# Two-layer hybrid decoder: the first loads on two DMA queues, and expert matrices read in one run per partition

## The chip, the cores and the metric

The kernel runs on one core of one Trainium2 chip. The metric is the device time of one execution in microseconds (us), from the runs listed below. The profile is one further execution, recorded by the hardware profiler. The engines are TensorE (PE, its weight loads PEld), VectorE (DVE), ScalarE (ACT), GpSimd (POOL) and SyncE (SP). SP, ACT and POOL each have a queue of their own into the core's 16 DMA engines, shown as q1, q10 and q0 in the profile.

## What is computed

Two layers over 512 tokens of 1024 features, all float32. Each layer has a mixer (sliding-window attention and an mLSTM, fed by one input projection) and a mixture of experts: 16 experts with 512 hidden features each, two of them per token. Both halves are preceded by a norm that a conditioning vector `c` modulates.

```python
mod = silu(c) @ ada_w[l] + ada_b[l]
sh1, sc1, g1, sh2, sc2, g2 = split(mod, 6)
h = rms_norm(x, norm_mix_w[l]) * (1.0 + sc1) + sh1
...                                    # mixer: x = x + g1 * (merged @ w_out[l])
h2 = rms_norm(x, norm_ffn_w[l]) * (1.0 + sc2) + sh2
# router: best group, then the best 2 experts e in it, weights gate
y = (silu(h2 @ w_gate[l, e]) * (h2 @ w_up[l, e])) @ w_down[l, e]
x = x + g2 * sum_over_2_experts(gate * y)
```

## The kernel before

Everything is written out by hand for each engine, with semaphores between them.

**The head** (before the loop over layers). SP issues the vector `c`, the positions and the router bias (L413 to L416), the first 2 MB block of `ada_w` (`load_head(0)`, L419), the router's matrix in two pieces (L429), then `params(0)`: 18 small loads through `rows` (L391), and then `x` (L431), the three other blocks of `ada_w` (L419) and the matrices of the `q` and `kv` projections (L424). ACT issues nothing here. DVE waits for all five constants (`const_in`), works out sine and cosine arguments (L1337 to L1359), ACT takes their sines (L666), then the silu of `c` (L669), and then squares and scales the four token tiles of `x` (L673, L678). PE transposes `c` (L948), waits for DVE and ACT, and in `param_columns(0)` waits for all 18 parameter loads, transposes the parameter rows (L967) and goes through `head_mods`: for each of four blocks of `ada_w` a product (L979), whose row ACT copies (L694) and whose columns PE sums (L961). Then the modulated tiles are transposed (L1020) and the `q` products start (L1030).

**The mixer** streams further blocks of `ada_w` through DVE (L1452, L1454); their sums are turned into columns on PE, for the chunks 6 to 9 by `paired_sums` (L955, four products of 128 columns). After the output projection (L1208) DVE writes the normed tokens `xn` (L1698), PE transposes them (L1216), and the router follows.

**The experts.** Tokens are scattered by expert into rows in DRAM and processed in blocks of 64 rows; an expert has one block or more. For a block PE does gate and up products (L1260), the transposes of the next block's rows (L1252), the down product of the block before (L1272) and the transposes of the hidden rows (L1266). DVE multiplies silu(gate) by up (`hx`, L1821) and scales the result (`y_row`, L1808). ACT issues the loads of the rows of later blocks (L887, 256 KB) and the stores of the result (L898, two of 128 KB). There are three buffers of weights: SP issues gate (L484) and up (L487) of expert e once the last gate and up product of expert e-3 is done, and POOL issues down (L617, or L619 and L620) once its last down product is done. Each is 2 MB:

```python
wait_reg(sp, gu_ready, blocks_through(sp, e - BUF))
load_gate(p, e)
load_up(p, e)
...
dve.wait_ge(y_out, b * 32 + 32)     # y_row of block b: the store of block b - 1 has landed
```

Gate and up are laid out by pairs of features (`of_pairs`): a partition holds four runs of 4 KB, 512 KB apart in DRAM. Down is laid out by `of`: four rows of 4 KB, also 512 KB apart. `wo` denotes the output projection, `gb` and `yb` gate and up products of the mLSTM branch.

## Time and profile before

| | |
|---|---|
| median of 3 runs | 1703.74 us (1700.13 to 1704.67) |
| the profiled execution | 1704.2 us, its span 1702.6 us |
| PE busy | 1488.8 us (87%) |
| DVE, ACT, POOL busy | 642.8, 324.3, 126.8 us |
| mean granted PE clock | 0.944 |
| DMA | 383.34 MB, 225 GB/s over the span |
| blocks of 64 rows | 46 in both layers |

How to read it: busy PE is not PE at its peak, and the share is a mean over stages with different limits. The head (0 to 51 us) and parts of the expert stages (553 to 848 and 1374 to 1677 us) are where PE waits for transfers; "granted clock" is PE's, 1.00 for 2.4 GHz and 0.50 for 1.2 GHz.

### The profile page before, as it was taken

How to read it: one execution, taken by the hardware profiler on the slowest of the kernel's cores; microseconds unless marked ns; L12 is line 12 of the kernel's file. 1: busy time of each engine (PE TensorE's matmuls, PEld its weight loads, DVE VectorE, ACT ScalarE, POOL GpSimd, SP SyncE). 2: the span in 40 equal slices, each digit the busy share in tenths (PEclk: the TensorE clock that was granted, in tenths of full speed). 3: DMA queues.
4: the chain of work that ended last, by engine and by line, in shares of the span. 5: the costliest groups of instructions: out<-in, count | busy, mean ns of one | idle time of the engine just before them, and what ended most of it. 6: DMA issues, size and time to landing. Idle time of an engine off the chain costs nothing.

```text
span 1702.6 us, 18332 instructions
## 1 busy us (share of the span) xinstructions
PE 1488.8 (87%) x5723; PEld 666.5 (39%) x5724; DVE 642.8 (38%) x1573; ACT 324.3 (19%) x825; POOL 126.8 (7%) x165
## 2 busy tenths in 40 slices
PE   2999999989992899989759999999999558999993
PEld 0544445544441333323234444454444223333331
DVE  1346434557524122112144554365763411121223
ACT  3223421100001112112143242111000111121220
POOL 1100000001102000000031000000110110000002
PEclk9999999999996799999979999999999869999997
DMA  8961112367706699999766012126773479996895
GB/s 265 386 249 49 51 50 84 114 249 294 279 18 247 183 347 392 379 389 390 267 236 221 1 50 86 62 99 232 262 253 142 152 271 381 392 387 230 304 383 181
DMA packets 140466, 383.34 MB, mean 225 GB/s; under 512 B 18760, under 2 KB 20984, under 8 KB 140408
## 3 DMA queue, kind: packets, MB, share of 16 engines
q1 hardware_dynamic: 107224, 273.04, 44.0%
q0 software_dynamic: 21664, 83.89, 13.1%
q10 hardware_dynamic: 11520, 25.70, 4.9%
q8 instruction: 29, 0.48, 0.1%
q14 instruction: 29, 0.24, 0.0%
HBM read 346.95 MB, written 35.65 MB: 225 GB/s over the span
## 4 chain that ended last, share of the span: by engine, by line
PE 74%; DMA 10%; DVE 5%; issue 5%; ACT 2%; POOL 1%; SPq 1%; POOLq 0%; ACTq 0%; DVEq 0%
PE bank L1041 23%; PE bank L1260 17%; PE bank L1030 11%; PE bank L1272 8%; PE bank L1208 5%; DMA weight_ring<-in_w_up_dram 4%; DMA regA<-in_w_up_dram 2%; PE bank L1252 1%; DMA h_features<-in_ada_w_dram 1%; DMA expert_rows<-merged_features 1%; PE bank L1108 1%; SPq L391 1%; PE bank L1266 1%; PE bank L1097 1%; POOL expert_rows L636 1%
## 5 line engine op out<-in xcount | busy, mean ns | idle before, releaser
L1041 PE MATMUL bank<-h_features,weight_ring 128*128 128x512 f32 x768 | 345.2, 603 | 2.0 <-ACT regB L756 2.0
L1260 PE MATMUL bank<-weight_ring,merged_features 128*64 128x512 f32 x960 | 224.9, 623 | 14.6 <-DMA weight_ring<-in_w_up_dram 7.5
L1041 PEld LDWEIGHTS bank<-h_features,weight_ring 128*128 128x128 f32 x768 | 146.7, 194 | 183.8 <-issue 183.5
L1030 PE MATMUL bank<-weight_ring,h_features 128*128 128x512 f32 (+1 forms) x512 | 196.3, 541 | 0.7 <-DVE h_features L1403 0.7
L1821 DVE TENSOR_TENSOR merged_features<-bank,merged_features 64x512 f32<-64x512 f32 x44 | 30.5, 693 | 364.2 <-ACT merged_features L890 364.2
L1030 PEld LDWEIGHTS bank<-weight_ring,h_features 128*128 128x128 f32 x512 | 95.9, 190 | 94.8 <-issue 90.7
L1260 PE MATMUL bank<-h_features,merged_features 128*64 128x512 f32 x256 | 116.7, 610 | 18.0 <-DMA regA<-in_w_up_dram 17.0
L1260 PEld LDWEIGHTS bank<-weight_ring,merged_features 128*64 128x64 f32 x960 | 72.1, 143 | 143.6 <-issue 138.9
L1272 PE MATMUL bank<-weight_ring,merged_features 128*64 128x512 f32 x528 | 120.6, 598 | 1.6 <-DVE merged_features L1808 1.6
L1260 PE MATMUL bank<-regA,merged_features 128*64 128x512 f32 x256 | 117.2, 612 | 0.0
L1208 PE MATMUL bank<-weight_ring,merged_features 128*128 128x512 f32 x256 | 114.3, 608 | 3.0 <-POOL merged_features L614 3.0
L890 ACT ACTIVATE merged_features<-bank 64x512 f32<-64x512 f32 x46 | 27.1, 590 | 351.3 <-PE bank L1260 351.3
L1208 PEld LDWEIGHTS bank<-weight_ring,merged_features 128*128 128x128 f32 x256 | 49.5, 195 | 64.7 <-issue 61.5
L881 ACT ACTIVATE merged_features<-bank,mod_cols,scale 128x64 f32<-128x64 f32 x192 | 62.2, 404 | 63.4 <-PE bank L1252 61.2
L1252 PE MATMUL bank<-ident,merged_features 64*128 64x64 f32 x384 | 34.9, 233 | 43.3 <-DMA merged_features<-expert_rows 43.3
L1260 PEld LDWEIGHTS bank<-h_features,merged_features 128*64 128x64 f32 x256 | 34.7, 141 | 80.5 <-issue 80.5
L1808 DVE TENSOR_TENSOR merged_features<-bank,g_rows 128x512 f32<-128x512 f32 x46 | 31.8, 691 | 88.0 <-PE bank L1272 83.0
L1804 DVE TENSOR_SCALAR merged_features<-bank,scale,mod_cols 128x64 f32<-128x64 f32 x192 | 52.8, 337 | 31.9 <-PE bank L1252 30.3
L1252 PEld LDWEIGHTS bank<-ident,merged_features 64*128 64x128 f32 x384 | 28.2, 142 | 80.8 <-DMA merged_features<-expert_rows 43.5
L1041 PE MATMUL bank<-regB,weight_ring 128*128 128x512 f32 x128 | 57.9, 595 | 1.6 <-DVE regB L1672 1.6
L1272 PEld LDWEIGHTS bank<-weight_ring,merged_features 128*64 128x64 f32 x528 | 35.4, 136 | 60.1 <-issue 58.0
L1041 PE MATMUL bank<-regA,weight_ring 128*128 128x512 f32 x128 | 57.7, 594 | 0.0
(319 smaller groups left out, 1456.6 us busy)
## 6 DMA issues: line engine op xcount, KB each, us to landing
weight_ring<-in_w_gate_dram SPq DMA_DIRECT2D x22, 2048.0 KB, 12.7
weight_ring<-in_w_up_dram SPq DMA_DIRECT2D x22, 2048.0 KB, 18.9
weight_ring<-in_w_down_dram POOLq DMA_DIRECT2D x22, 2048.0 KB, 16.7
weight_ring<-in_w_in_dram SPq DMA_DIRECT2D x18, 2048.0 KB, 17.7
x_tokens<-in_ada_w_dram SPq DMA_DIRECT2D x14, 2048.0 KB, 8.0
h_features<-in_w_gate_dram SPq DMA_DIRECT2D x10, 2048.0 KB, 11.4
regA<-in_w_up_dram SPq DMA_DIRECT2D x10, 2048.0 KB, 20.2
regA<-in_ada_w_dram SPq DMA_DIRECT2D x8, 2048.0 KB, 8.0
```

The source lines that it names most:

```text
L391: sp.dma_start(dst, src).then_inc(params_in, 16)
L881: last = ac.activation(xT[:, k, :], ps[2][:, MB * k:MB * k + MB], ACT.Identity, scale=A2[:, k:k + 1], bias=modc[:, 24 + k:25 + k])
L890: ac.activation(hsil[64:P, :], ps[3][0:64, :], ACT.Silu).then_inc(sil_ready, 1)
L1030: ins = te.matmul(bank[:, 0:w], hT[:, k, P * i:P * i + P], wv[:, k, :], start=(k == 0), stop=(k == KD - 1))
L1041: ins = te.matmul(bank[:, :], wv[:, k, c0:c0 + P], rhs[:, k, :], start=(k == 0), stop=(k == kn - 1))
L1208: ins = te.matmul(bank[:, :], merged[:, k, P * i:P * i + P], slot(f"wo{k // 4}", 4, D)[:, k % 4, 512 * h:512 * h + 512], start=(k == 0), s ...
L1252: ins = te.transpose(ps[(2, 6)[k % 2]][:, MB * k:MB * k + MB], xg[p][:, P * k:P * k + P], ident[MB * p:MB * p + MB, MB * p:MB * p + MB])
L1260: ins = te.matmul(ps[3][64 * part:64 * part + 64, :], xT[:, k, :], w[:, k, :], start=(k == 0), stop=(k == KD - 1))
L1272: ins = te.matmul(ps[5][64 * half:64 * half + 64, :], hxT[:, k, :], down_w[p][k][:, 512 * half:512 * half + 512], start=(k == 0), stop=(k ...
L1804: last = ve.tensor_scalar(xT[:, k, :], ps[6][:, MB * k:MB * k + MB], A2[:, k:k + 1], modc[:, 24 + k:25 + k], ALU.mult, ALU.add)
L1808: ve.tensor_tensor(yb, ps[5][:, :], g2bc[:, :], ALU.mult).then_inc(y_taken, 1)
L1821: ve.tensor_tensor(hx, ps[3][64:P, :], hsil[64:P, :], ALU.mult).then_inc(hx_ready, 1)
```

## The change

It has four parts. First, in the head, SP issues only `c`, the four blocks of `ada_w`, `q` and `kv`; ACT issues the positions, `x`, the router bias, the router's matrix and the parameters, 16 loads now, before its own first activation. Second, gate, up and down are read so that partition p holds the K consecutive rows pK to pK+K-1 of the matrix: one run of 16 KB (down of buffer 1: runs of 12 and 4 KB). Third, what is multiplied by them is written in the same order: `hx` with a stride of 4 elements on both inputs, `xn` with a stride of 8 (it was 2), and the columns of the modulation in chunks 6 to 9 by eight products of 64 columns. Fourth, the parameters of the second norm are loaded as columns straight away (three loads of 128 x 8), so the transposed rows are 68 and not 128.

```diff
-        def of_pairs(w, l, e):
-            return w.rearrange("l e (m p r) f -> (l e) p m (r f)", p=P, r=2)...
+        def whole_rows(w, l, e, k):
+            return w.rearrange("l e (p k) f -> (l e) p (k f)", k=k)[bass.ds(l * E + e, 1)].rearrange("a p n -> p (a n)")
...
-            load_head(0)
-            sp.wait_ge(zeroed, 2)
-            for r in range(2):
-                sp.dma_start(rwz[:, r:KD:2, 0:E], router_w.rearrange("(m p r) e -> p m r e", p=P, r=2)[:, :, r, :])...
-            params(0)
-            sp.dma_start(xs[:, :, :], x.rearrange("a (i p) d -> p (a i) d", p=P)).then_inc(x_in, 16)
-            for j in range(1, HEAD_ADA):
+            for j in range(HEAD_ADA):
                 load_head(j)
             for name in ("q", "kv"):
                 load(0, name)
...
-                    sp.dma_start(gate_w[p].rearrange("p (m r) n -> p m (r n)", r=2), of_pairs(w_gate, l, e))...
+                    sp.dma_start(gate_w[p].rearrange("p k n -> p (k n)"), whole_rows(w_gate, l, e, KD))...
...
-                        po.dma_start(ring[:, (2, 1, 5)[p], :].rearrange("p (k n) -> p k n", k=FC), of(w_down, l, e))...
+                        po.dma_start(ring[:, (2, 1, 5)[p], :], whole_rows(w_down, l, e, FC)).then_inc(w_dn[p], 16)
...
         def _(act):
             ac = nc.scalar
 
+            with nc.allow_non_contiguous_dma(reason="positions by token"):
+                act.dma_start(rt[:, 0:NT].bitcast(I32), positions...).then_inc(const_in, 16)
+            act.dma_start(xs[:, :, :], x.rearrange("a (i p) d -> p (a i) d", p=P)).then_inc(x_in, 16)
+            act.dma_start(rbias[:, :], router_bias...).then_inc(const_in, 16)
+            act.wait_ge(zeroed, 1)
+            act.dma_start(rwz[:, :, 0:E], router_w.rearrange("(p k) e -> p k e", p=P)).then_inc(const_in, 16)
+            params(act, 0)
             act.wait_ge(dve_const, 1)
             ac.activation(sinr[:, :, :]...
...
+            def row_column_sums(bank, half, rows):
+                for k in range(KD):
+                    ins = te.matmul(bank[64 * half:64 * half + 64, k:k + 1], rows.rearrange("t (p k) -> t k p", k=KD)[:, k, :],
+                                    ones[:, 0:1], start=True, stop=True)
...
-                    ve.tensor_scalar(xn[:, i, :].rearrange("t (m r p) -> t m r p", r=2, p=P), xs[:, i, :].rearrange("t (m p r) -> t m r p", p=P, r=2),
+                    ve.tensor_scalar(xn[:, i, :].rearrange("t (k p) -> t k p", p=P), xs[:, i, :].rearrange("t (p k) -> t k p", k=KD),
                                      rs[:, 4 + i:5 + i], None, ALU.mult).then_inc(xn_ready, 1)
...
+                def hidden():
+                    by_row = lambda a: a.rearrange("t (p k) -> t k p", k=FC)
+                    ve.tensor_tensor(hx.rearrange("t (k p) -> t k p", p=P), by_row(ps[3][64:P, :]), by_row(hsil[64:P, :]), ALU.mult).then_inc(hx_ready, 1)
```

On SP, at the start of the program, before the change (`regP`, `rbias` and `router_padded` take the constants, `weight_ring` and `h_features` the blocks of `ada_w`):

```order
L413 DMA regP<-in_c_dram 8x128
L415 DMA regP<-in_positions_dram 128x4x1
L416 DMA router_bias<-in_router_bias_dram 128x16
L419 DMA weight_ring<-in_ada_w_dram 128x8x512
L429 DMA router_padded<-in_router_w_dram 128x4x16 x2
L391 DMA regP<-in_norm_mix_w_dram 8x128
...
L391 DMA gate_columns_padded<-in_w_in_dram 128x8x4 x2
L431 DMA x_tokens<-in_x_dram 128x4x1024
L419 DMA weight_ring<-in_ada_w_dram 128x8x512 x2
L419 DMA h_features<-in_ada_w_dram 128x8x512
```

And the same place of SP after it:

```order
L406 DMA regP<-in_c_dram 8x128
L410 DMA weight_ring<-in_ada_w_dram 128x8x512 x3
L410 DMA h_features<-in_ada_w_dram 128x8x512
L415 DMA weight_ring<-in_w_in_dram 128x8x512
L415 DMA weight_ring<-in_w_in_dram 128x8x256
```

All constants but `c`, `x` and every parameter have left SP, so that the four blocks of `ada_w` follow each other at once.

On ACT, the start of the program after the change (before it ACT began with the table load and the sine, and issued nothing):

```order
L649 DMA regP<-in_positions_dram 128x4x1
L650 DMA x_tokens<-in_x_dram 128x4x1024
L651 DMA router_bias<-in_router_bias_dram 128x16
L653 DMA router_padded<-in_router_w_dram 128x8x16
L381 DMA regP<-in_norm_mix_w_dram 8x128
...
L381 DMA g_rows<-in_ada_b_dram 128x1024
L381 DMA qk_norm_rows<-in_q_norm_w_dram 128x64
...
L381 DMA param_cols<-in_ada_b_dram 128x8 x2
...
L381 DMA gate_columns_padded<-in_w_in_dram 128x8x4 x2
L656 ACT_TABLE_LOAD
L656 ACTIVATE sin<-regP 128x32
```

`x` now stands ahead of the router's matrix and of all parameters, and ACT's first activation behind all of these issues.

## Rows read from the trace of the kernel before

**Rows 1.** Busy time by stretch, 10 to 20 us; last: clock, DMA share, GB/s.
```profile
10.00:20.00 10.00, 0.27 (x1) 0.18 (x1) 5.28 (x35) 1.82 (x4) 0.00 (x0) 1.00 0.58 73
```

**Rows 2.** Timeline of the head: start, us, engine, line, tiles, [idle before <-releaser].
```profile
11.26 0.17 DVE L1337 CAST regP<-regP 128x4 f32<-128x4 int32 x1 [11.26 <-DMA router_padded<-in_router_w_dram]
...
18.04 1.52 SPq L431 DMA_DIRECT2D x_tokens<-in_x_dram  x1
...
20.60 0.45 PE L967 MATMUL bank<-ident,regP 128*128 128x128 f32 x1 [9.05 <-DMA gate_columns_padded<-in_w_in_dram]
...
21.49 3.64 PE L979 MATMUL bank<-weight_ring,c_padded 128*32 128x512 f32 x16 [0.44 <-DVEq L1391]
...
27.00 1.06 ACT L673 ACTIVATE merged_features<-x_tokens 128x1024 f32<-128x1024 f32 x1 [8.74 <-DMA x_tokens<-in_x_dram]
...
36.52 1.05 PE L961 MATMUL bank<-ones,regU 128*128 128x1 f32 x8 [0.44 <-ACT regU L694]
...
37.87 1.92 PE L979 MATMUL bank<-weight_ring,c_padded 128*32 128x512 f32 x16 [0.30 <-DMA weight_ring<-in_ada_w_dram]
...
43.30 3.39 PE L979 MATMUL bank<-h_features,c_padded 128*32 128x512 f32 x16 [2.51 <-DMA h_features<-in_ada_w_dram]
```

**Rows 3.** The chain that ended last: start, us, what.
```profile
51.08 7.10 PE bank L1030 x16
...
712.25 3.58 PE bank L1272 x16
```

**Rows 4.** DMA queues, 18 to 21 us, SP's queue with short packets: packets, MB, share.
```profile
q1 hardware_dynamic: 2316, 0.12, 64.0%
```

**Rows 5.** DMA queues, 30 to 40 us, SP's queue alone with runs of 2 KB.
```profile
q1 hardware_dynamic: 1920, 3.87, 105.1%
```

**Rows 6.** DMA queues, 749 to 751 us, runs of 4 KB: SP's, then POOL's.
```profile
q1 hardware_dynamic: 104, 0.43, 53.3%
q0 software_dynamic: 96, 0.39, 49.1%
```

**Rows 7.** DMA queues, 778 to 779 us, ACT's queue with stores of 2 KB.
```profile
q0 software_dynamic: 43, 0.18, 42.8%
q1 hardware_dynamic: 39, 0.16, 38.9%
q10 hardware_dynamic: 43, 0.09, 22.6%
```

**Rows 8.** PE's waits, experts of layer 1 and then 2: us in total, times, longest.
```profile
PE bank L1260 <- DMA regA<-in_w_up_dram: 10.2, 2, 7.9
PE bank L1260 <- DMA weight_ring<-in_w_up_dram: 7.5, 2, 5.9
...
PE bank L1260 <- DMA regA<-in_w_up_dram: 6.7, 1, 6.7
```

**Rows 9.** SP's timeline of issues, and the landing time of the issue at 793.74.
```profile
641.65 0.38 SPq L484 DMA_DIRECT2D weight_ring<-in_w_gate_dram  x1
...
793.74 8.35 SPq L487 DMA_DIRECT2D weight_ring<-in_w_up_dram  x1
...
weight_ring<-in_w_up_dram SPq DMA_DIRECT2D x1, 2048.0 KB, 35.4
...
1389.38 0.38 SPq L484 DMA_DIRECT2D weight_ring<-in_w_gate_dram  x1
```

**Rows 10.** The chain that ended last, layer 2: the wait for up of expert 5.
```profile
1414.78 33.68 DMA regA<-in_w_up_dram
```

**Rows 11.** Timeline, two blocks: result rows and ACT's stores.
```profile
739.38 0.69 DVE L1808 TENSOR_TENSOR merged_features<-bank,g_rows 128x512 f32<-128x512 f32 x1 [1.78 <-PE bank L1272]
...
740.32 1.13 ACTq L898 DMA_DIRECT2D expert_rows<-merged_features  x2
...
751.02 0.69 DVE L1808 TENSOR_TENSOR merged_features<-bank,g_rows 128x512 f32<-128x512 f32 x1 [1.79 <-PE bank L1272]
```

**Rows 12.** One line's instructions: ns min/median/max, first and last start.
```profile
L1698 DVE TENSOR_SCALAR regA<-x_tokens,rstd x8: 752/754/754, 471.8 to 1335.6; 128x1024 f32<-128x1024 f32 x8
```

More of the change, by code:

```diff
@@ L424, in load @@
                 sp.dma_start(dst, src).then_inc(item_in[name], 16)
-            load_head(0)
-            sp.wait_ge(zeroed, 2)
-            for r in range(2):
-                sp.dma_start(rwz[:, r:KD:2, 0:E], router_w.rearrange("(m p r) e -> p m r e", p=P, r=2)[:, :, r, :]).then_inc(const_in, 16)
-            params(0)
-            sp.dma_start(xs[:, :, :], x.rearrange("a (i p) d -> p (a i) d", p=P)).then_inc(x_in, 16)
-            for j in range(1, HEAD_ADA):
+            for j in range(HEAD_ADA):
                 load_head(j)
@@ L945, in _ @@
             te = nc.tensor
-            pe.wait_ge(const_in, 16 * 5)
+            pe.wait_ge(const_in, 16 * 4)
             pe.wait_ge(pool_const, 2)
@@ L950, in _ @@
             pe.wait_ge(dve_const, 3)
-            def paired_sums(bank, rows):
-                for q in range(4):
-                    ins = te.matmul(bank[:, q:q + 1], paired(rows, q), ones[:, 0:1], start=True, stop=True)
-                return ins
             def column_sums(bank, rows):
@@ L962, in column_sums @@
                 return ins
+            def row_column_sums(bank, half, rows):
+                for k in range(KD):
+                    ins = te.matmul(bank[64 * half:64 * half + 64, k:k + 1], rows.rearrange("t (p k) -> t k p", k=KD)[:, k, :],
+                                    ones[:, 0:1], start=True, stop=True)
+                return ins
             def param_columns(t):
-                wait_head(pe, params_in, t, 18 * 16, 18 * 16)
-                te.transpose(ps[2][:, 0:P], prm[:, :], ident[:, :]).then_inc(param_cols, 1)
+                wait_head(pe, params_in, t, 16 * 16, 16 * 16)
+                te.transpose(ps[2][:, 0:68], prm, ident[0:68, 0:68]).then_inc(param_cols, 1)
             def head_mods():
```

92 lines of the change are left out of this document (42 added, 50 removed).

## The prediction, made before the change was run

> **What bounds the kernel now.** I read the busy time by stretch first, then the chain that ended last, then the timeline of the head and PE's waits in the experts, and last the DMA queues. From 10 to 20 us PE works 0.27 us and DMA moves 73 GB/s [rows 1]: the short parameter loads fill SP's queue. PE's first real work waits for the last of them at 20.6 us, and later steps wait for `x` (27.0) and for blocks of `ada_w`, the fourth at 43.3 [rows 2]; the `q` products start at 51.08 [rows 3]. That is the first place. The second is the experts: a block takes 11.64 us of PE (from 739.38 to 751.02) [rows 11], and where experts with one block follow each other their 6 MB come too late. PE waits 17.7 us in layer 1 and 6.7 in layer 2 for an up matrix [rows 8]. Between these places the mixer is PE's own, and no part of the change reaches it but the column sums.
>
> **Prices of packets.** With SP's queue alone and runs of 2 KB, 1920 packets take 105.1% of 160 us, 87.6 ns each [rows 5]. Runs of 4 KB take 53.3% of 32 us over 104, 164 ns each [rows 6]. On a straight line through both, a packet of 16 KB takes 622 ns against 4 x 164 = 656: 5.1% less per byte. Packets under 512 B: 64.0% of 48 us over 2316, 13 ns each [rows 4]. Two queues get one packet each in turn (104 and 96) [rows 6], three as well (43, 39, 43), although ACT's are of 2 KB there and the others of 4 [rows 7]. So the turn goes by packets, not by bytes.
>
> **The head.** Before, 18 parameter loads and the router's 2 stood ahead of `x` and three blocks. Now SP's queue has the four blocks at once, 64 packets of 2 KB for each block and engine, and ACT's has the rest. What was one queue of 13 ns packets is now one whose every packet takes a turn with a 2 KB packet: 88 + 13 = 101 ns. I count ACT's packets for each of 16 engines, from the shapes in the order shown: `x` 32 of 4 KB; then router bias 8, router matrix 64 (128 x 8 pieces), parameter rows 4, `g1` 8 of 4 KB, the two norms 16, sinks 8, three columns 24, gate columns 128. `x` is issued at about 1.5 us; before, it took from 18.04 to 27.0 us for 32 x 0.164 = 5.2 us of packets, so some 2 us go by before its first packet. From 3.5 us: `x` 32 x (0.088 + 0.164) = 8.1; the 260 others x 0.101 = 26.3, plus 1.2 for the 4 KB ones, plus about 2, an estimate, for one short packet that ends each load, plus 1 to be seen: parameters complete at **42 us**, against 20.6 [rows 2]. If a 13 ns packet slips in beside the long one for nothing, 260 x 0.088 gives 38.5; if every landing is as late as `x`'s was, 44. I take 42.
>
> The fourth block has landed by then: all that goes before it is 256 x 0.0876 + 5.2 for `x` + 1.3 + some 4 of short ones + 3.5 + 1 = 37.8 us. The constants end behind 72 of ACT's turns, near 20 us (before 11.3), and DVE's 5 us after them still end before 42. ACT issues until about 30 us and then has its sines, a table load and 9 us of squares and scaling, which also ends near 42. So the chain from the parameters on decides: 0.9 to the first block's product, 3.64, then about 2.9 for the second (3.64 on the low clock, 1.92 on the high), a column sum 1.0, third 1.92, column sum 1.0, and from the start of the fourth 7.8 - 1.5 = 6.3 (51.08 - 43.30, less 3.39 - 1.92) [rows 2, 3]: 17.7 us. `q` starts at 59.8: **+8.7 us**. Bounds +5 and +11.
>
> **The experts.** SP's queue in layer 1 is filled from 641.65 on: each later pair is issued before the pair ahead has landed, up to the up matrix issued at 793.74, which lands at 829.1 [rows 9]. 5.1% of these 187.5 us is 9.6. In layer 2 the same holds from 1389.38 to 1448.5 [rows 9, 10]: 3.0. Gain 12.6 us, of the 24.4 waited. As ends: nothing, if packets gain nothing, and 31 us, all of the waits and an estimate of 7 for the products behind them that run at the low clock (3.64 against 1.92 for the same product) [rows 2].
>
> Some is given back. By turns, ACT's rows pay for the long packets: a block has 4 packets of loaded rows, 8 of stores and 3 that end a load or store, per engine, 15 turns. With SP and POOL both full, a turn is 2 x 0.622 us, and 15 take 18.7 + 1.4 us against the block's 11.64; with SP alone 10.7. `y_row` waits for the store of the block before. The store is issued at 740.32, the next `y_row` came at 751.02 [rows 11] and could slip to about 758 before PE's down product waits: 17 us of slack, of which 4 go by before a first packet. Its 9 turns take 11.9 us with both full, 7.1 with one, and loaded rows can stand ahead. POOL's 32 packets of 4 KB per expert, each beside one of SP's, fill 32 x 0.328 = 10.5 us of the 16.7 that an expert takes (46 blocks over 32 experts, 11.64 each), so I take 5.6 us given back, and 0 and 17 as ends. **-7.0 us** in sum, bounds -31 and +5.
>
> **The rest.** `xn` reads with a stride of 8 elements. With stride 2 the 1024 elements took 754 ns [rows 12], faster than one per DVE cycle; I take half a microsecond more, for the last tile of each layer (the others hide under the output projection): +1.0, bounds 0 and +2. The Trainium skill, SBUF — State Buffer, on cachelines (16 bytes there, 8 in PSUM, a line to be hit twice), speaks against all strided reads here; by it the 0.754 us could double, +1.5 in sum, and no row here has such a stride. The `hx` product hides under PE's down product of 3.58 us [rows 3], in which ACT's silu and DVE's evacuation of the next block's rows (both about a microsecond) lie too; so it could take some 1.5 to 2 us more, and costs 0. The column sums, 8 calls, have twice the products of half the columns, 1.05 us before [rows 2]: 0, and 0 and +7 as ends. The next layer's parameters lose their 4-byte pieces in the shadow of the experts: 0; if SP were late there, gate of expert 3 would come later.
>
> **Sum:** +8.7 - 7.0 + 1.0 = +2.7 on 1704.2 (span 1702.6 and 1.6 around it) is 1706.9. The median of the runs stands 0.5 lower, so **1706.5 us**. A measurement of this kernel tells 0.3%, 5.1 us, from no change.
>
> **Rivals.**
> *Short packets don't take a turn each.* If a queue gives several short ones per turn, parameters are in at about 26 us and the fourth block at 37.8 decides instead of 43.3: -5.5. With -7.0 and +1.0 that is 1692.5. For it: nothing shows short packets in turn with long ones. Against: ACT's 2 KB stores got one per turn, not two for one of 4 KB [rows 7]. The Trainium skill, DMA: Bandwidth & Descriptors, "Queues, rings and completion order", says an engine drains a whole packet of typically 9 to 17 descriptors before it switches; by that this rival would hold. Rows 7 don't bear it out for 2 KB.
> *Rows starve behind long packets* (the other side). If 16 KB gain nothing (656 ns), the turn with both queues full is 1.31 us, the store needs 4 + 9 x 1.4 = 16.6 of its 17 us, and any loaded rows ahead of it make `y_row` late in most blocks from 641 to 829 us. It decides once a turn passes 1.4 us. Experts +5, head +8.7, rest +1: 1718.
> *The runs are not one packet.* If the queue cuts 16 KB into packets of 4 as before, nothing moves in the experts: +8.7 + 1.0, 1713.5. Against: no run here was longer than 4 KB, so nothing either way.
>
> **How the numbers follow.** Forecast 0.50, first rival 0.28, second 0.13, third 0.09. The forecast's own range is -4 to +12: 0.04 faster, 0.30 within 0.3%, 0.16 slower. The first rival is faster but for 0.01 (0.27); the second and third are slower but for 0.01 of the third. Sums: faster 0.31, same 0.32, slower 0.37. For 8 in 10 the range reaches 5.5 us below the first rival and just past the second: 1687 to 1719, with some 0.1 left out on either side.
>
> **What would show it.** Right: the parameters' transpose between 38 and 44 us with DMA near 390 GB/s from 4 us on, the first `q` product at 57 to 62; packets of 16 KB in the queues, about 620 ns each; the up waits smaller, DVE idle before `y_row` on DMA. Wrong: a transpose before 30 us (first rival); waits of `y_row` above 5 us in sum beside unchanged waits for up (second); no packet above 4 KB (third). If `hx` takes over 2.5 us, a term I left at nothing is the bound of every block, and the prediction fails.

## The result, and the profile after

Four runs of the changed kernel took 1743.12 us in the median (1737.07 to 1744.21), beside 1703.57 us for the kernel before on the same chip: ratio 1.0228, 95% interval 1.0201 to 1.0256. It is 39 us slower, where 1706.5 had been forecast and 1719 was the upper end. The profiled execution, the fastest of the four, took 1737.07 us, span 1735.5, granted clock 0.947.

The span is 32.9 us longer. Cut at PE's first product of each stage, it lies here (us; in brackets PE's granted clock over the stage):

| stage, up to | before | after | difference |
|---|---|---|---|
| head, first `q` product | 51.1 | 58.0 | +6.9 |
| mixer 1, first output product | 401.2 (0.99) | 406.9 (0.98) | +5.7 |
| router 1, first gate product | 106.9 | 106.3 | -0.6 |
| experts 1, first transpose of layer 2 | 309.0 | 313.2 | +4.2 |
| mixer 2 | 405.8 (0.98) | 411.4 (0.97) | +5.6 |
| router 2 | 105.8 | 104.6 | -1.2 |
| experts 2, end | 322.8 | 335.1 | +12.3 |

Each column is one execution, and stages scatter. Over these two profiles and those of the experiments that share the code of a stage, the experts took 304.3 to 309.0 us before and 310.3 to 314.6 after in layer 1, and 321.5 to 322.8 and 334.4 to 336.9 in layer 2; `q` started at 51.1 to 54.5 us before and at 57.7 to 59.0 after.

**The head** is close to the forecast. The timeline of the head after the change (start, us, engine, line, tiles, idle before and its releaser):

```profile
21.37 0.17 DVE L1328 CAST regP<-regP 128x4 f32<-128x4 int32 x1 [21.37 <-DMA router_padded<-in_router_w_dram]
...
41.69 0.35 PE L958 MATMUL bank<-ident,regP 68*128 68x68 f32 x1 [20.02 <-DMA gate_columns_padded<-in_w_in_dram]
...
42.41 5.47 PE L970 MATMUL bank<-weight_ring,c_padded 128*32 128x512 f32 x32 [0.38 <-DVEq L1382]
...
57.96 2.38 PE L1021 MATMUL bank<-weight_ring,h_features 128*128 128x512 f32 x5 [0.71 <-ACT h_features L674]
```

The parameters' transpose starts at 41.69 us (20.60 in [rows 2]; 42 forecast), `q` at 57.96 (59.8 forecast). The two queues in this time (packets, MB, share of 16 engines), 20 to 30 us and then 30 to 40:

```profile
q1 hardware_dynamic: 1506, 3.02, 83.7%
q10 hardware_dynamic: 1505, 0.63, 24.6%
...
q1 hardware_dynamic: 1735, 3.48, 98.3%
q10 hardware_dynamic: 1676, 0.03, 11.7%
```

ACT's packets, of some 20 bytes each in the second stretch (0.03 MB in 1676), take turns one for one with SP's of 2 KB. Equal counts over 10 us could also come of equal groups. But in three stretches of 0.21 us from 34.00 us on (two turns of each of the 16 engines) the two queues moved 38 and 38, 34 and 34, 39 and 40 packets; with groups of nine or more these counts would scatter by a dozen (an estimate). The Trainium skill, DMA: Bandwidth & Descriptors, "Queues, rings and completion order", has an engine drain a whole packet of typically 9 to 17 descriptors before it switches. The trace does not agree: these counts show single turns, and refute the first rival.

**The experts.** PE's waits for up matrices (24.4 us in [rows 8]) are gone. DVE waits in their place; its largest wait for transfers (us in total, times, longest), and then all DMA from 640 to 830 us, before and after:

```profile
DVE merged_features L1804 <- DMA expert_rows<-merged_features: 147.3, 20, 13.9
...
DMA packets 20391, 73.55 MB, mean 387 GB/s; under 512 B 1299, under 2 KB 1299, under 8 KB 20391
...
DMA packets 8445, 73.35 MB, mean 386 GB/s; under 512 B 1225, under 2 KB 1225, under 8 KB 4419
```

L1804 is `y_row`, which waits for the store of the block before: 147.3 us over 20 blocks, against 4.9 us once before. From 714 to 716 us a packet of 16 KB takes 0.61 us (29 packets fill 55.4% of 32 us), as I had extrapolated:

```profile
q1 hardware_dynamic: 29, 0.48, 55.4%
q0 software_dynamic: 22, 0.36, 42.0%
...
q1 hardware_dynamic: 64, 1.05, 84.7%
q10 hardware_dynamic: 64, 0.26, 19.9%
```

From 706 to 710 us, though, where ACT's queue loads rows and POOL's is empty, the same packet takes 0.85 us. So the rate over the filled stretch did not rise by the forecast 5.1%: it is 386 GB/s, before 387. In this stretch of layer 1 DMA is full in both kernels, and one wait was exchanged for another. In the first 120 us of the experts of layer 2 the rate fell, from 364 to 355 GB/s. The chain that ended last, after the change, layer 1, shows what a block is made of (start, us, what):

```profile
705.53 0.70 DVE merged_features L1804
...
707.12 15.47 DMA expert_rows<-merged_features
722.61 0.70 DVE merged_features L1804
...
724.21 17.35 DMA expert_rows<-merged_features
741.58 0.70 DVE merged_features L1804
```

`y_row`, its store, the store's landing, the next `y_row`: a ring of 17.1 and 19.0 us, where a block of [rows 11] took 11.64. The chain has eleven such rounds in the two layers, of 13.6 to 19.2 us; their stores took 12.0 to 17.6 us to land.

**Blocks that wait for no transfer** are longer too. The chain in layer 2 after the change:

```profile
1634.61 0.39 PE bank L1257 x4
1635.00 0.45 issue
1635.45 7.09 PE bank L1251 x32
```

Two in three of these blocks take 12.0 to 12.2 us, the others 11.75. Their 0.3 to 0.49 us of "issue", in which PE waits for nothing that the profile shows, were 0.15 at most before (a third of the blocks at 11.77 us, the others at 11.63).

**The strided operations and the mixer.** One line each (ns min/median/max, first and last start): `hx` before and after, then `xn`, then the weight loads of the column sums; and one call of these on the timeline of the mixer, before and after; last, PE over a stretch behind another call (us, PE busy, granted clock, DMA share, GB/s):

```profile
L1821 DVE TENSOR_TENSOR merged_features<-bank,merged_features x44: 692/693/695, 583.8 to 1668.8; 64x512 f32<-64x512 f32 x44
...
L1801 DVE TENSOR_TENSOR merged_features<-bank,merged_features x46: 1045/1080/1102, 580.9 to 1703.1; 64x512 f32<-64x512 f32 x46
...
L1690 DVE TENSOR_SCALAR regA<-x_tokens,rstd x8: 1142/1150/1156, 484.4 to 1355.7; 128x1024 f32<-128x1024 f32 x8
...
L951 PEld LDWEIGHTS bank<-ones,regU x96: 194/217/220, 287.8 to 1178.3; 128*64 128x64 f32 x96
...
280.85 1.00 PE L955 MATMUL bank<-ones,regU 128*128 128x1 f32 x8
...
287.80 2.08 PE L951 MATMUL bank<-ones,regU 128*64 128x1 f32 x16
...
1179.40:1182.80 3.40, 3.40 (x5) 0.50 0.00 0
```

`hx` takes 1.08 us (0.69 before), `xn` 1.15 (0.754 in [rows 12]). A column sum takes 2.08 us; before, with four products of 128 columns, it took 1.00 (each product is two instructions). Eight sums make 8.6 us of the 11.3 that the mixers grew by. The granted clock has the rest: PE was at its low level for 13.6 us of each mixer, before for 10.2. The fall at 1179.4 us comes 0.8 us behind a column sum. Twice 3.4 us at half speed are 3.4 us, an estimate, so 12.0 us together.

### The profile page after: what moved, and what is told of

It is laid out like the page before. It is cut to its first block, busy times and chain, and to the rows that moved or that the text cites. A ratio compares the mean times of both kernels' runs of the same rounds, so it can differ in the third digit from the quotient of the medians.

```text
span 1735.5 us, 18454 instructions
## 1 busy us (share of the span) xinstructions
PE 1502.1 (87%) x5787; PEld 687.0 (40%) x5788; DVE 663.8 (38%) x1573; ACT 323.9 (19%) x825; POOL 119.3 (7%) x164
## 4 chain that ended last, share of the span: by engine, by line
PE 70%; DMA 13%; issue 6%; DVE 6%; ACT 2%; POOL 2%; ACTq 1%; POOLq 0%; DVEq 0%
PE bank L1032 23%; PE bank L1251 14%; PE bank L1021 11%; DMA expert_rows<-merged_features 10%; PE bank L1263 7%; PE bank L1199 5%; DMA gate_columns_padded<-in_w_in_dram 1%; PE bank L1243 1%; ACTq L381 1%; PE bank L1099 1%; DMA regA<-expert_rows,slot_index 1%; PE bank L1088 1%; PE bank L951 1%; DVE merged_features L1804 1%; POOL expert_rows L619 1%
## 5 line engine op out<-in xcount | busy, mean ns | idle before, releaser
L1801 DVE TENSOR_TENSOR merged_features<-bank,merged_features 64x512 f32<-64x512 f32 x46 | 49.7, 1081 | 290.0 <-ACT merged_features L880 290.0
L1251 PEld LDWEIGHTS bank<-weight_ring,merged_features 128*64 128x64 f32 x960 | 79.1, 140 | 133.0 <-issue 129.2
L1804 DVE TENSOR_TENSOR merged_features<-bank,g_rows 128x512 f32<-128x512 f32 x46 | 31.8, 691 | 184.2 <-DMA expert_rows<-merged_features 147.3
L1263 PEld LDWEIGHTS bank<-weight_ring,merged_features 128*64 128x64 f32 x528 | 38.7, 144 | 83.0 <-issue 81.3
L1032 PE MATMUL bank<-regA,weight_ring 128*128 128x512 f32 x128 | 61.2, 623 | 0.0
## 6 DMA issues: line engine op xcount, KB each, us to landing
weight_ring<-in_w_in_dram SPq DMA_DIRECT2D x18, 2048.0 KB, 12.7
```

The lines of the kernel that those rows point to most:

```text
L1032: ins = te.matmul(bank[:, :], wv[:, k, c0:c0 + P], rhs[:, k, :], start=(k == 0), stop=(k == kn - 1))
L1251: ins = te.matmul(ps[3][64 * part:64 * part + 64, :], xT[:, k, :], w[:, k, :], start=(k == 0), stop=(k == KD - 1))
L1263: ins = te.matmul(ps[5][64 * half:64 * half + 64, :], hxT[:, k, :], down_w[p][k][:, 512 * half:512 * half + 512], start=(k == 0), stop=(k ...
L1801: ve.tensor_tensor(hx.rearrange("t (k p) -> t k p", p=P), by_row(ps[3][64:P, :]), by_row(hsil[64:P, :]), ALU.mult).then_inc(hx_ready, 1)
L1804: ve.tensor_tensor(yb, ps[5][:, :], g2bc[:, :], ALU.mult).then_inc(y_taken, 1)
```

## The experiments

Each ran beside the kernel before. Differences between experiments are differences of these ratios, times 1703.6 us; by their intervals such a difference is uncertain by 6 to 10 us. "After" is the changed kernel.

**The head put back.**

```diff
...
+            load_head(0)
+            sp.wait_ge(zeroed, 1)
+            sp.dma_start(rwz[...], router_w...)
+            params(sp, 0)
+            sp.dma_start(xs[...], x...)
-            for j in range(HEAD_ADA):
+            for j in range(1, HEAD_ADA):
```

(positions and router bias ahead of these, and all of them taken off ACT)

> Only the head is put back: positions, router bias, router matrix, the 16 parameter loads and x go to SP again, in the order of before, and ACT issues nothing there. Theory (parameters are late because each short packet of ACT's takes a turn with a 2 KB packet of SP's): the parameters' transpose comes at 18 to 22 us and not at 41.7, q starts at 50 to 52 us and not at 57.96, and the whole gets 7 us shorter than after, since nothing behind the head sees it: about 1736. Rival (the head costs nothing in the end, because what is late there is made up in the mixer, whose weights come no sooner): q is earlier but the time stays within 2 us of after's.

Measured 1732.67 us, ratio 1.0181 (1.0149 to 1.0214): 8.0 us less than after. The parameters' transpose came at 18.55 us and `q` at 46.71, earlier than before's 51.08. By 20 us SP's queue had moved 6378 packets, before's 8708; that this is why was not tested. The 11.3 us by which `q` is earlier than after's came out as 8, so most of what the head loses stays lost, as forecast.

**All short loads first, on both queues.**

```diff
             sp.dma_start(crow, ...)
...
+            params(sp, 0, (0,))          # rows, norms, sinks, three columns
             for j in range(HEAD_ADA):
...
-            act.dma_start(xs[...], x...)
             act.dma_start(rbias...); act.dma_start(rwz...)
-            params(act, 0)
+            params(act, 0, (1,))         # gate columns, gate biases, g1
+            act.dma_start(xs[...], x...)
```

> After, but in the head all short loads stand ahead of the long ones on both queues: SP c, the parameter rows, norms, sinks and the three columns, then the four blocks of ada; ACT positions, router bias, router matrix, gate columns, gate biases, g1, then x. Theory (turns): while only short packets are in both queues a turn costs 2 x 13 ns, the parameters are complete at 8 to 12 us, the fourth block at 35 to 37, q starts at 44 to 46 us, 12 to 14 less than after's: about 1730. Rival (short loads cost by the load, some microseconds each to land, not by the turn): parameters not before 20 us, q not before 50, at most 8 us less.

Measured 1727.61 us, ratio 1.0145 (1.0113 to 1.0178), 14.1 us less than after. The timeline of its head:

```profile
11.92 0.38 PE L962 MATMUL bank<-ident,regP 68*128 68x68 f32 x1 [5.81 <-ACT c_padded L663]
...
22.08 3.45 PE L974 MATMUL bank<-weight_ring,c_padded 128*32 128x512 f32 x16 [9.78 <-DMA weight_ring<-in_ada_w_dram]
```

The parameters are there by 11.92 us, while short packets only meet short ones; PE then waits 9.78 us for the first block of `ada_w`. `q` starts at 46.48 (at 44.4 to 49.9 in the three profiles below that have this head and 16 KB packets). The turn theory holds.

**Packets of 4 KB in the changed layout.**

```diff
-  sp.dma_start(gate_w[p]..., whole_rows(w_gate, l, e, KD)).then_inc(w_gu[p], 16)
+  for b in range(2):
+      sp.dma_start(every_other(gate_w[p]..., b), every_other(whole_rows(w_gate, l, e, KD), b)).then_inc(w_gu[p], 16)
```

(up and down likewise, counts doubled)

> After, but gate, up and down are each read by two DMAs that take every other 4 KB, so that no packet is over 4 KB; layout, strides and head stay. Theory (the result rows wait for the store because each of its packets, and of the loads of rows ahead of it, waits out a 16 KB packet of SP's and one of POOL's): the waits of y_row for the store fall from 147 us to under 20, PE's waits for up matrices come back (15 to 30 us), experts of layer 1 take about 312 us from first gate to first K of the next layer instead of 315.7, those of layer 2 about 12 us less, the whole 15 to 18 us less: about 1726. Rival (the late store comes of the rows' own loads, which keep all queues at 330 GB/s whatever the length of the others' packets): waits of y_row stay over 100 us and the time within 4 us of after's.

Measured 1735.96 us, ratio 1.0203 (1.0150 to 1.0255): only 4 us less, with intervals that overlap, where 15 to 18 were expected. But the waits changed places as the theory said. PE's and DVE's waits for transfers in this run (us in total, times, longest):

```profile
PE bank L1260 <- DMA regA<-in_w_up_dram: 15.0, 2, 10.2
...
DVE merged_features L1813 <- DMA expert_rows<-merged_features: 9.5, 2, 5.0
...
PE bank L1260 <- DMA weight_ring<-in_w_up_dram: 8.5, 2, 4.6
```

From 147.3 us to 9.5 for `y_row`, and 23.5 us for up matrices. Packet length is what makes the store late (it lands in 6.7 us here, in the median). The time hardly followed: PE's waits for matrices are back, and blocks without any wait still took 12.0 us, a second cause beside the first.

**Two buffers for the result rows.**

```diff
-        yb = mflat[:, 3072:3584]
+        yb = [mflat[:, 3072:3584], mflat[:, 3584:4096]]
...
-                    dve.wait_ge(y_out, b * 32 + 32)
+                    with dve.If(b % 2 == 0):
+                        wait_reg(dve, y_out[0], (b // 2) * 32 + 32)
```

> After, but with two buffers for the result rows of a block, so that y_row waits for the store of two blocks before (11.6 us more slack). Theory (only the store is late, loaded rows have slack enough): waits of y_row fall from 147 us to under 40, a block falls from 17 us towards 12 to 14, DMA comes close to 440 GB/s and PE's waits for weights are smaller than before's 24 us; the whole is 15 to 25 us less, 1718 to 1728. Rival (everything that ACT's queue moves is late in the same measure): the waits move to PE's transposes of the next block's rows (L1252), and the time stays within 5 us of after's. A second rival (DMA as a whole is the bound and y_row's waits lie beside it): waits of y_row vanish, PE's waits for up and gate take their place in the same sum, again within 5 us.

Measured 1721.10 us, ratio 1.0119 (1.0087 to 1.0151): 18.6 us less than after, the largest single term; the expert stages are 14.2 us shorter in the profile. Landing times in this run, 640 to 840 us (KB, median us): loads of rows, then stores.

```profile
merged_features<-expert_rows ACTq DMA_DIRECT2D x16, 256.0 KB, 17.0
expert_rows<-merged_features ACTq DMA_DIRECT2D x31, 128.0 KB, 15.9
```

A store takes 15.9 us to land, still, and rows 17.0 (7.2 before). With two buffers the ring may take two blocks; 50.2 us of `y_row`'s waits and 12.7 us more of PE's waits for rows are left.

**Three tests of the longer block.** In the traces of before and after PE's first gate product of a block comes 2.8, 3.1 or 3.2 us after the end of `hx`, where nothing else is late. First, `hx` without strides and PE's transposes reading every fourth column:

```diff
-  ve.tensor_tensor(hx.rearrange("t (k p) -> t k p", p=P), by_row(ps[3][64:P, :]), by_row(hsil[64:P, :]), ALU.mult)
+  ve.tensor_tensor(hx, ps[3][64:P, :], hsil[64:P, :], ALU.mult)
...
-  ins = te.transpose(ps[4][...], hx[:, P * k:P * k + P], ident[0:MB, 0:MB])
+  ins = te.transpose(ps[4][...], hx.rearrange("t (p k) -> t k p", k=FC)[:, k, :], ident[0:MB, 0:MB])
```

> After, but DVE writes hx without strides and PE's four transposes take every fourth column of it instead. In the traces, PE's first gate product of a block starts 1.97 to 2.1 us after DVE's last evacuation of that block's rows, before and after the change alike, and that evacuation stands behind hx on DVE. Theory (this chain sets a block's length, so that hx's 1.10 instead of 0.70 us adds 0.39 us to each): hx takes 0.69 us again, blocks that wait for no transfer fall from 12.02 to 12.15 us back to 11.63 to 11.78, about 26 of them, so 9 to 12 us less than after: 1731 to 1734. Rival (the gap on PE comes of something else in the changed program, such as its instruction stream): blocks stay at 12.0 and the time within 3 us of after's. Should PE's strided weight loads be slower than 138 ns, the transposes of 0.46 us show it.

Measured 1734.32 us, ratio 1.0162 (1.0118 to 1.0206), 11 us less. Blocks take 11.87 us: no "issue" is left, but the transposes' weight loads went from 138 ns to 215:

```profile
L1257 PEld LDWEIGHTS bank<-ident,merged_features x184: 192/215/217, 585.4 to 1707.0; 64*128 64x128 f32 x184
```

`hx` takes 0.69 us again. That the 11 us lie within the 9 to 12 expected was luck in part: the theory had PE wait for the evacuation, which the next two runs refute, and a shorter `hx` helps by either account.

Second, `xt_dve()`, the evacuation of the next block's rows, moved ahead of `hidden()` on DVE; once in after, once in before:

```diff
+                    dve.wait_ge(xt_ready, b + 3)
+                    xt_dve()
                     dve.wait_ge(sil_ready, b + 2)
                     dve.wait_ge(ht_ready, b + 1)
                     hidden()
-                    dve.wait_ge(xt_ready, b + 3)
-                    xt_dve()
```

> After, but DVE evacuates the transposed rows of the next block before it works out hx; nothing else. Theory (PE waits for that evacuation, then its sequencer needs 1.97 us to the first gate product): the evacuation ends 1.1 us earlier, the gap between the hidden rows' transposes and the first gate product falls from 0.77 to 0.39 us or less, blocks to about 11.6 us or a little under, the whole 9 to 14 us less than after. Rival (PE waits for hx, 3.1 us ahead of the gate product, and not for the evacuation): hx now ends 0.7 us later, blocks grow by up to 0.7 us to 12.7 and the whole by 15 us or more.

> The kernel before, with the same exchange: DVE evacuates the next block's transposed rows before it works out hx. Theory (the same chain already sets the block before the change: the gap there is 0.39 to 0.54 us): the gap falls to 0.1 us or less, blocks from 11.63 to about 11.3 us, and, since the stretches that wait for weights take part of it back, 5 to 12 us less than before: 1692 to 1699. Rival (PE's own work fills the block before the change, the 0.39 being its transposes' own length and nothing to win): within 2 us of before.

Measured 1765.79 us, ratio 1.0366 (1.0319 to 1.0412), and 1722.98, ratio 1.0122 (1.0092 to 1.0151). The theory that PE waits for the evacuation fell in both. The chain of the first of the two:

```profile
1640.74 0.39 PE bank L1257 x4
1641.13 1.38 issue
1642.51 7.09 PE bank L1251 x32
```

The "issue" grew by the 1.1 us that `hx` now ends later; the distance from `hx` to the gate product stayed 2.83 to 3.24 us in both kernels, that from the evacuation did not. So PE waits for `hx`, and what follows is most likely its sequencer, since no engine is waited for there. Third, therefore, the wait for `hx` and the transposes behind it moved to the start of the next round, behind the loop's end and two register loads; in after and in before:

```diff
-                h_transposes(0)
                 with pe.Fori(0, nb1) as b:
                     e1 = te.value_load(tabs[0:1, bass.ds(b + 1, 1)], ...)
                     e0 = te.value_load(tabs[0:1, bass.ds(b, 1)], ...)
+                    h_transposes(b)
...
-                    h_transposes(b + 1)
+                h_transposes(nb1)
```

> After, but in PE's loop over blocks the transposes of a block's hidden rows, and the wait for hx ahead of them, stand at the start of the next round, behind the two register loads of the expert numbers, instead of at the end of the round. The order of PE's work is the same. In all traces so far 2.83, 3.11 or 3.24 us pass from the end of hx to the next gate product. Theory (they pass in PE's sequencer: loop, register loads, waits and branches that it can only reach behind the wait for hx): with the register loads ahead of the wait the time falls by at least the 0.38 us that hx grew by, the gap between transposes and gate product goes from 0.77 to 0.91 back to 0.39 us, blocks from 12.02 to 12.15 to 11.6 us, and the whole is 9 to 12 us less than after. Rival (the 3.1 us are in the branches behind the waits, not in the loads): blocks stay above 11.9 and the time within 3 us of after's.

> The kernel before with the same move of the wait for hx behind PE's register loads. Theory: a third of its blocks (those of the buffer whose branch lies deepest) have a gap of 0.52 instead of 0.39 us, which goes: 0.13 x 15, 2 us less than before, 1701, not to be told from it by the time, only by the gap; no block gets shorter than 11.6. Rival (the loads were not hidden at all before): blocks to 11.3 us and 8 us or more less.

After: 1736.43 us, ratio 1.0192 (1.0162 to 1.0222), 6.1 less, with intervals that overlap; the expert stages of the profile are 8.8 us shorter. Its chain has no "issue" left, and blocks of 11.63 us although `hx` takes 1.08:

```profile
1626.31 0.39 PE bank L1257 x4
1626.69 7.02 PE bank L1251 x32
```

The kernel before so edited: 1699.72 us, ratio 0.9999 (0.9984 to 1.0015), all blocks that wait for no transfer at 11.63. There `hx` had 0.1 us of slack or none, but this cost nothing that shows in the time.

**The column sums.** First, half of each sum's products left out (half of the columns of the second norm's shift and scale are missing in what is computed):

```diff
-                for k in range(KD):
+                for k in range(KD // 2):
```

> After, with four of the eight products in each column sum of chunks 6 to 9; half of the columns of the second norm's shift and scale are left out of the computation. Theory (a product of 64 columns costs PE as much as one of 128, and the sums lie on PE's path in the mixer): 2.01 us per call falls to about 1.0, eight calls, each mixer 4.2 us shorter, the whole 8.5 us less than after. Rival (they lie beside PE's waits in the mixer): under 2 us less.

Measured 1784.56 us, ratio 1.0478 (1.0447 to 1.0509). Without these columns tokens went to other experts, in 49 blocks and not 46, so the time says nothing; the first mixer alone was 3.3 us shorter. Second, the kernel before with each product split in two of 64 columns:

```diff
                 for q in range(4):
-                    ins = te.matmul(bank[:, q:q + 1], paired(rows, q), ones[:, 0:1], ...)
+                    for h in range(2):
+                        ins = te.matmul(bank[64 * h:64 * h + 64, q:q + 1], paired(rows, q)[:, 64 * h:64 * h + 64], ones[:, 0:1], ...)
```

> The kernel before, with each of the four products of a column sum of chunks 6 to 9 split in two of 64 columns, as many products as after has. Theory (a product of one column costs PE about 0.25 us whether its weights have 128 or 64 columns, and these sums lie on PE's path): 0.95 us per call becomes 1.9 to 2.1, 8 calls, each mixer 4 us longer, the whole 8 to 9 us more than before, 1710. Rival (the mixer's own waits hide them): under 3 us more.

Measured 1700.18 us, ratio 0.9991 (0.9975 to 1.0007): nothing, against my theory. Line and timeline:

```profile
L956 PEld LDWEIGHTS bank<-ones,regU x96: 135/138/139, 282.1 to 1154.2; 128*64 128x64 f32 x96
...
282.10 0.65 PE L956 MATMUL bank<-ones,regU 128*64 128x1 f32 x16
```

As many products as after has, of the same size, in 0.65 us and not 2.08. What differs is the stride at which the weights are read, 2 elements here and 8 there. Third, after with three of four sums put in order by DVE's last step, so that the products read neighbours:

```diff
+   elif k == KD - 1 and n < N_HALVED:
+       link(ve.scalar_tensor_tensor(sums_by_k.rearrange("t (k p) -> t k p", k=KD), by_k(w[:, k, :]), cz[:, k, 0:1], by_k(acc), ...))
...
+   one = rows.rearrange("t (p k) -> t k p", k=KD)[:, k, :] if rows is not None else sums_by_k[:, 64 * k:64 * k + 64]
```

> After, but DVE's last multiply-add of three of the four row sums (chunks 6 to 8) writes them by k into the free half of the buffer, so that PE's eight products of such a sum load 64 neighbouring columns; the fourth (chunk 9) stays as it is. In the split run of before, 16 matmuls (8 products) of 64 columns at a stride of 2 took 0.65 us, in after at a stride of 8 they take 2.08. Theory (the stride of the weight load is the price, not the number of products, and it lies on PE's path): 0.65 us for six of the eight calls, less some 0.4 us each on DVE for the strided last step, which lies beside PE: 8.6 us less than after, 1734 to 1736. Rival (PE's sums lie beside DVE's chain in the mixer): within 3 us of after.

Measured 1728.84 us, ratio 1.0143 (1.0124 to 1.0162): 14.5 us less than after. On the timeline a sum in order takes 1.09 us, the one left as it was 2.08:

```profile
343.44 1.09 PE L955 MATMUL bank<-ones,regU 128*64 128x1 f32 x16
382.30 2.08 PE L955 MATMUL bank<-ones,regP 128*64 128x1 f32 x16
```

Six calls by 0.99 us are 5.9; the mixers were 2.9 and 7.5 us shorter in the profile. The second has more to it by the clock: PE was at the low level for 3.4 us of it and not 13.6. The 10.2 us at half speed are up to 5.1, an estimate, and with the 3.0 of three sums 8.1. In the first mixer both kernels have 13.6. The other profiles bear this out in part. Between the first and the last of a mixer's four sums the clock falls once or twice in all 11 kernels of this document with strided sums, in both mixers, for 3.4 us nearly each time, and each fall starts from 0.8 us ahead to 1.3 us behind a sum's end. It never falls there in the five with before's layout, with half of the products, or with sums in order (two kernels). Elsewhere in the mixers the low stretches vary from run to run.

**All mended places together.** Short loads first, two result buffers and the later wait for `hx`; the same once more beside a twin with 4 KB packets; and with the sums in order as well:

> After with three edits at once: short loads first in the head, two buffers for the result rows, and the register loads ahead of the wait for hx. Theory (three terms that lie at different places add up): 22 us for the two buffers, 15 for the head, 9 to 12 for the loads, so about 1695, 8 us less than before, in spite of the column sums' 8.5. Rival (with shorter blocks the stretches that wait for DMA get longer, since the same bytes come in less time): of the last term a third to a half is lost, 1700 to 1703, the same as before.

> The kernel with the three edits (short loads first, two result buffers, wait for hx behind the register loads) once more, beside its twin with 4 KB packets. Expected as measured: 1700 to 1708.

> The kernel with the three edits, but gate, up and down in packets of 4 KB (every other 4 KB in one of two DMAs). Over 700 to 830 us DMA moved 386 GB/s in the profile with 16 KB packets and 387 in that of before: higher where only matrices are moved (420 to 425 against 393 to 409), lower where rows are (322 to 384 against 360 to 388). Theory (16 KB packets gain nothing over the filled stretch, what they win alone they lose beside the rows): the same time as its twin within 4 us. Rival (my price, 622 ns for 16 KB against 656 for four of 4 KB, holds, and with the waits for the store gone it shows): the twin with 16 KB is 8 to 12 us faster. Second rival (16 KB cost in sum): the twin is over 5 us slower.

> The kernel with three edits (short loads first, two result buffers, wait for hx behind the register loads) and this fourth one. Its twin with three came to 1703.3 and 1705.9 us, 1.0011 and 1.0014 of before. Theory: 8.6 us less than the twin, 1695 to 1697, ratio 0.996, so a little faster than before and 2.8% faster than after. Rival (the shorter mixer brings no earlier experts, since the first three experts' matrices are loaded by then, but the later ones are not): half of it is given back, 1699 to 1701, the same as before.

| | us | ratio | interval |
|---|---|---|---|
| three places | 1705.93 | 1.0014 | 0.9983 to 1.0045 |
| the same again | 1703.29 | 1.0011 | 0.9986 to 1.0037 |
| its twin, 4 KB packets | 1721.30 | 1.0102 | 1.0067 to 1.0137 |
| four places | 1696.66 | 0.9961 | 0.9936 to 0.9985 |

Of three places the rival held: level with before, not 8 us under it. The last beats both kernels: 0.4% under before, 2.6% under after, and 8.5 us under its twin with three places, as expected. The twin in 4 KB packets is 15.5 us slower (by the intervals 8 to 23), on the side of the first rival but more than its 8 to 12. Its waits, and those of the run beside it:

```profile
PE bank L1272 <- DMA weight_ring<-in_w_up_dram: 14.5, 4, 5.5
PE bank L1272 <- DMA regA<-in_w_up_dram: 14.2, 2, 11.0
```

```profile
DVE merged_features L1818 <- DMA expert_rows<-merged_features: 40.6, 7, 7.9
DVE merged_features L1821 <- DMA expert_rows<-merged_features: 38.1, 6, 10.6
```

Over 640 to 830 us DMA moved 388 GB/s in the twin and 387 in the other. The expert stages together took 632.4 against 624.4 us, 8 of the 15.5; the mixers were 10 us longer, at granted clocks of 0.97 for 0.98, though the edit does not touch them; PE was at the low level for 37.4 us of them and for 27.2 in the other. And the four kernels with before's layout and order of DVE, in 4 KB packets and one DMA per matrix, took 624.6 to 631.8 us for both stages, 627.4 in the mean; the three mended kernels in 16 KB packets 627.3, 624.4 and 619.6, 623.8 in the mean. By these means the 16 KB packets gain some 4 us, less than either group scatters, by the twin 8 in these stages. Which of the two holds stays open, since the twin also has twice the DMAs.

**The head and the wait in the kernel before**, with its own layout: short loads first on both queues (as above), the wait for `hx` moved.

> The kernel before with the layout of before throughout (4 KB runs, hx and xn as they were, four products per column sum), but with the head's short loads first on both queues and the wait for hx moved. Theory: q starts at 45 to 47 us instead of 51.1, of which the mixer gives back 1 to 2 us (its matrices come from the same queues, and in the two kernels with an early q it was 1.5 to 3 us longer), and 2 us of the move: 4 to 6 us less than before, 1697 to 1699. Rival (the mixer gives all of it back): within 2 us of before.

Measured 1700.33 us, ratio 0.9999 (0.9986 to 1.0013). `q` started at 52.4 us, no earlier than before. The chain shows what stands ahead of it (SP's issues of parameter loads, then of the first block of `ada_w`):

```profile
6.06 3.00 SPq L389
9.10 6.48 SPq L389
...
18.29 0.43 SPq L420
```

The second norm's parameters come in 4-byte pieces there; their last two issues take 3.00 and 6.48 us, and SP comes to the first block at 18.29 us (6.32 in the run with short loads first). So the order was not tried in the sense of the theory, and whether the mixer gives an early `q` back stays open. Loading these parameters as columns, the fourth part of the change, is by this what makes the order pay.

## Why the prediction was wrong, step by step

The sum put +8.7 us on the head, -7.0 on the experts and +1.0 on the rest. The profiles have +6.9, +16.5 and +9.5. The experts are the term that failed, and in it the store's way back.

- **The head, +8.7: right** within its bounds. Parameters at 41.69 (42), `q` 6.9 us later. The run that puts it back gains 8.0, with a `q` 4.4 us earlier than before's. Two blocks' products took 5.47 us, not 6.5.
- **The price of a 16 KB packet, -12.6: too large.** 0.61 us is what it costs where matrices meet matrices, but 0.85 beside loads of rows, and the rate over the filled stretch is 386 GB/s, before 387. The waits for up matrices are gone as forecast, but not because the matrices come faster: the blocks ask for them later.
- **"I take 5.6 us given back": the step that failed most.** No working leads to the 5.6; it was chosen between 0 and 17. The landing was sized rightly, 4 + 11.9 = 15.9 us against a measured 12.0 to 17.6. It was held against 17 us of slack as if `y_row` were late once. But each store waits on the `y_row` before it and each `y_row` on the store before it, so this ring must fit into a block's 11.64 us every time; the slack absorbs one lateness, not a row of them. With my own numbers the block would have been 15.9 + 0.9 (from the start of `y_row` to the store's issue) = 16.8 us wherever both queues are full; 13.6 to 19.2 were measured. Two buffers take 18.6 us back, and the run with short packets showed that the waits vanish with the packets' length. This is the second rival's mechanism, and its condition that long packets gain nothing is nearer to the measured rate than my 5.1%; but a turn stayed at 2 x 0.61 us and not over 1.4, and its 1718 was too low because it too counted slack once.
- **"`hx` could take some 1.5 to 2 us more, and costs 0": wrong.** It took 0.39 more and lengthened two blocks in three by that, the others by 0.12. The cover I named, PE's down product, hides the work but not PE's sequencer, which stands at the wait for `hx` and then has 2.83 to 3.24 us of its own before the next gate product. With the wait behind the loop's end and two register loads the blocks are back at 11.63 us; in time this is 6.1 us, not clear of the noise, in the expert stages 8.8. The sign of being wrong that I gave, `hx` over 2.5 us, never came: it takes 1.08.
- **The column sums, 0 with +7 as an end: the wrong end.** They cost 8.6 us (8 by 1.08), by the stride and not by the number of products, to which I had given them; the falls of the clock behind them come on top.
- **`xn`, +1.0: right** in size (0.40 us more for each of two last tiles, bounds 0 and +2); no run tests what it costs in time. On strides, the Trainium skill, SBUF — State Buffer, "Specifications (TRN2)", wants two hits in a line of 16 bytes for full bandwidth. The trace agrees in the direction: at strides of 8 and 4 elements the two DVE operations took 1.5 to 1.6 times as long, not the twice that I had worked out.
- The first rival (several short packets to a turn) and the third (runs cut into 4 KB) are refuted by the queues' counts.
- Small sums: what goes before the fourth block adds up to 37.4 us and not 37.8, the first rival to 1692.3; ACT's silu takes 0.59 us and not about one; POOL's packets, 32 of 4 KB in the working, are 8 of 16 KB. None of these decides anything.

The single edits take back 8.0 + 18.6 + 6.1 + 14.5 = 47 us, more than the 39 lost. Each of the four is uncertain by 6 to 7 us, the head of that run starts `q` earlier than before's did, and the last sum has clock in it; so no gain of the long packets can be read from the difference.

## What to carry to other kernels

Where a wait closes a ring (result, store, next result), compare the ring's length with the period, not with the slack of one round. An operation that seems hidden under another engine's work may still have a wait in front of that engine's register loads and branches: look for "issue" time behind it, and put such loads ahead of the wait. Where DMA is full in a stretch, a wait that goes there is replaced by another; look at the stretches where it is not full. A new layout is to be priced at every reader, also where PE loads weights: here the strides that the long runs asked for (8.6 us in the sums, 6 to 9 in the blocks) cost about as much as the ring that the long packets made too long (18.6).

## What was not expected of the hardware

- A weight load of 64 columns takes 138 ns at a stride of 1 or 2 elements and 217 at a stride of 8; with one-column products behind them 16 such take 0.65 us (stride 2), 1.09 (stride 1) and 2.08 (stride 8). The load itself takes the same at strides 1 and 2, so why the 16 take longer at stride 1 is open; the runs differ in more than that. 64-row transposes went from 138 to 215 ns at a stride of 4.
- A 16 KB packet takes 0.61 us from 714 to 716 us, beside POOL's of 16 KB and ACT's stores of 2 KB, and 0.85 from 706 to 710, beside ACT's loads of 4 KB rows alone. Why is open.
- PE's granted clock fell to the low level once or twice among the four strided sums of a mixer (2.08 us of one-column products each), mostly for 3.4 us, and never among sums of 0.65 to 1.12 us.
- From the end of `hx` to the next gate product 2.8 to 3.2 us passed, with four transposes, a loop end, two register loads, two waits and the branches in between. Of these the sequencer's share is inferred: no run splits them further.
